# Cache loads of a decoder step's sample attention issued by ScalarE's queue instead of SyncE's

## What is computed

```python
n   = rms_norm(x) @ w_in                      # 320 x 2048 @ 2048 x 4608, nine blocks of 512 columns
ya  = u * (tril(w_s) @ rms_norm(v))           # gMLP gate
yb  = window_attention(q, [cache_k, k], [cache_v, v], rel_bias)   # 16 heads x 64, three dilations mixed
ym  = memory_attention(qm, mk, mv)            # 4 heads x 128, 256 memory tokens
h   = x + concat(ya, yb, ym) @ w_out
y   = h + moe(rms_norm(h))                    # top-1 of 4 groups, top-2 of 8 SwiGLU experts in it
```

## Time and profile before

| | us |
|---|---|
| median of 3 runs | 1200.65 |
| the runs | 1200.0, 1200.65, 1203.96 |
| the profiled execution, its own time | 1201.35 |
| its span, first to last instruction | 1199.5 |
| mean granted TensorE clock | 0.963 |

### The profile page before, as it was taken

One profiled execution on the slowest core, in us unless ns is written; L12 is line 12 of the kernel. 1 busy time (PEld: TensorE's weight loads), 2 busy tenths in 40 slices (PEclk: granted clock), 3 DMA queues, 4 the chain that ended last, 5 costly groups with the idle time before them and its releaser, 6 DMA issues.

```text
span 1199.5 us, 17462 instructions
## 1 busy us (share of the span) xinstructions
PE 1076.0 (90%) x7153; PEld 593.7 (49%) x7153; DVE 534.4 (45%) x1046; ACT 212.0 (18%) x465; POOL 41.4 (3%) x38
## 2 busy tenths in 40 slices
PE   7996889998999999989999998898888878888876
PEld 3674667665676665767777542333222222222322
DVE  3573553556455455475354215334242433333323
ACT  1111011231122221231011023111211210101010
POOL 0030110001010000010000000000000000000000
PEclk9897899999999999999999999999999998999997
DMA  9987234898999998753773436999999999999994
GB/s 334 337 243 295 97 128 146 357 369 316 370 351 392 403 371 316 312 220 105 271 284 132 176 134 267 428 425 427 427 428 427 428 428 428 427 427 427 426 426 149
DMA packets 38751, 385.48 MB, mean 321 GB/s; under 512 B 4879, under 2 KB 7567, under 8 KB 10223
## 3 DMA queue, kind: packets, MB, share of 16 engines
q1 hardware_dynamic: 36112, 376.87, 78.6%
q0 software_dynamic: 1568, 5.62, 1.7%
q10 hardware_dynamic: 1008, 2.10, 0.5%
HBM read 376.67 MB, written 7.90 MB: 321 GB/s over the span
## 4 chain that ended last, share of the span: by engine, by line
PE 65%; DMA 20%; DVE 7%; issue 3%; ACT 3%; POOL 1%; DVEq 0%; SPq 0%; ACTq 0%; POOLq 0%
PE ps L594 22%; DMA arena<-w_gu 16%; PE ps L586 6%; PE ps L1007 5%; PE ps L1037 5%; DMA arena<-w_proj 4%; PE ps L990 4%; PE ps L1021 3%; PE ps L788 3%; PE ps L755 3%; PE ps L576 3%; PE ps L1014 2%; PE ps L1042 1%; POOL stat L1798 1%; PE ps L771 1%
## 5 line engine op out<-in xcount | busy, mean ns | idle before, releaser
L594 PE MATMUL ps<-arena 128*128 128x256 f32 x1456 | 343.0, 391 | 22.4 <-DMA arena<-w_proj 12.3
L594 PEld LDWEIGHTS ps<-arena 128*128 128x128 f32 x1456 | 276.5, 194 | 76.6 <-issue 28.3
L1007 PE MATMUL ps<-arena,cst 128*32 128x512 f32 x1024 | 130.4, 643 | 40.3 <-DMA arena<-w_gu 39.4
L1749 DVE STREAM_TRANSPOSE cst<-ps 128x512 f32<-128x512 f32 x31 | 22.2, 717 | 192.8 <-PE ps L990 192.8
L586 PE MATMUL ps<-arena 128*64 128x256 f32 x832 | 101.3, 385 | 0.0
L990 PE MATMUL ps<-arena 128*32 128x512 f32 (+1 forms) x768 | 95.7, 612 | 1.2 <-DVE arena L1698 1.2
L1007 PEld LDWEIGHTS ps<-arena,cst 128*32 128x32 f32 x1024 | 32.7, 114 | 128.5 <-issue 84.1
L1021 PE MATMUL ps<-arena,cst 128*32 128x512 f32 x512 | 68.1, 653 | 20.7 <-DVE cst L1751 20.7
L586 PEld LDWEIGHTS ps<-arena 128*64 128x64 f32 x832 | 55.1, 136 | 38.4 <-issue 14.8
L1767 DVE COPY arena<-ps 32x512 f32<-32x512 f32 x64 | 44.2, 691 | 51.9 <-PE ps L1021 51.0
L1292 DVE TENSOR_TENSOR arena<-arena 128x512 f32<-128x512 f32 x52 | 35.7, 687 | 67.7 <-PE ps L594 45.8
(11 more groups left out here) (262 smaller groups left out, 974.5 us busy)
## 6 DMA issues: line engine op xcount, KB each, us to landing
arena<-w_gu SPq DMA_DIRECT2D x64, 2048.0 KB, 32.6
arena<-w_dn SPq DMA_DIRECT2D x32, 2048.0 KB, 31.2
arena<-w_proj SPq DMA_DIRECT2D x43, 1024.0 KB, 7.8
arena<-kc SPq DMA_DIRECT2D x16, 2048.0 KB, 9.9
arena<-vc SPq DMA_DIRECT2D x16, 2048.0 KB, 9.7
arena<-w_o SPq DMA_DIRECT2D x16, 1024.0 KB, 4.9
arena<-kc SPq DMA_DIRECT2D x8, 1024.0 KB, 8.1
arena<-vc SPq DMA_DIRECT2D x8, 1024.0 KB, 9.6
```

The costliest lines, as they stand in the source:

```text
L594: last = mm(psum[:, regions(v)[j - 1]], left[a], right[:, a], start=first and opens and a == 0, stop=final and a == 1, skip_group_check=True)
L1007: last = mm(ps[g:g + 32, 0, :], xgT[:, s % 2, kt, :], gate_up[(3 * s + h) % RING][:, k, :], start=kt < 4, stop=kt >= KT - 4)
```

## The change

The functions keys and values move from SyncE's program into ScalarE's, with the same semaphores, sources, sizes and destinations; the 48 loads are issued by ScalarE's queue. In ScalarE's tile loop the calls stand behind sample_exp and sample_turned and ahead of the memory attention, head_turned and turned. Unit 0's three key loads are written at s = 5, behind a wait for the 16 pieces of the memory projection. SyncE keeps weights, biases, rows and expert weights, and loses the two waits (sumsq, unit_done) that stood ahead of unit 0's keys.

```diff
@@ SyncE's program
-            def keys(n, j):
-                if n:
-                    sp.wait_ge(spv_mm, 3 * n - 2 + j)
-                a = HP * sum(KEYS_P[:j])
-                sp.dma_start(kp[j], kc[n, :, a:a + HP * KEYS_P[j]]).then_inc(kv_loaded[j], 16)
-
-            def values(n, j):
-                sp.wait_ge(s_mm, 3 * n + j + 1)
-                a = HP * sum(KEYS_P[:j])
-                sp.dma_start(vp[j], vc[n, :, a:a + HP * KEYS_P[j]]).then_inc(kv_loaded[j], 16)
-
             sp.wait_ge(tab_out, 16)
             window_bias(0)
             window_bias(1)
             sp.wait_ge(rows_out, 16 * NQ)
             sp.wait_ge(dset, 2)
             sample_bias(0)
-            sp.wait_ge(sumsq, 5)
-            sp.wait_ge(unit_done, UNITS_M)
-            for j in range(3):
-                keys(0, j)

             for s in range(UNITS_X):
                 if s % 3 == 2:
                     sp.wait_ge(unit_done, UNITS_M + s + 1)
                     weights(11 + s // 3)
-                n, i = sample_step(s)
-                if n is not None and i <= 2:
-                    values(n, i)
-                if n is not None and i >= 4 and n + 1 < NUNIT:
-                    keys(n + 1, i - 4)
@@ ScalarE's program
+            def keys(n, j):
+                if n:
+                    act.wait_ge(spv_mm, 3 * n - 2 + j)
+                a = HP * sum(KEYS_P[:j])
+                act.dma_start(kp[j], kc[n, :, a:a + HP * KEYS_P[j]]).then_inc(kv_loaded[j], 16)
+
+            def values(n, j):
+                act.wait_ge(s_mm, 3 * n + j + 1)
+                a = HP * sum(KEYS_P[:j])
+                act.dma_start(vp[j], vc[n, :, a:a + HP * KEYS_P[j]]).then_inc(kv_loaded[j], 16)
+
             for s in range(UNITS_X):
+                if s == 5:
+                    act.wait_ge(unit_done, UNITS_M)
+                    for j in range(3):
+                        keys(0, j)
                 if s % 12 == 10:
                     evict_first(s // 12)
                 if s % 12 == 11:
@@
                 if n is not None and 3 <= i <= 5:
                     sample_turned(n, i - 3)
+                if n is not None and i <= 2:
+                    values(n, i)
+                if n is not None and i >= 4 and n + 1 < NUNIT:
+                    keys(n + 1, i - 4)
                 if s in (MEM_AT, MEM_AT + 2):
                     memory_exp((s - MEM_AT) // 2)
```

## The result

The changed kernel takes 1203.94 us in the median of 12 runs (1197.89 to 1205.36), the kernel before 1200.22 us in 12 runs beside them (1198.6 to 1203.96). The ratio is 1.0025, with a 95% interval of 1.0014 to 1.0036: slower by about 3 us, when 1198.65 was forecast and 1203.0 was the end of the range. The profiled execution has a span of 1203.0 us, 3.5 us over the one before.

The account below looks back on a forecast made before the run. PE bounds the kernel until the expert stage, where DMA does. A 2.7 us gain at chunk 11 less 0.7 us of issues gave -2.0 us: 1199.35 for the profiled execution, 1198.65 us as median; range 1187.5 to 1203.

Parts of the forecast that it names:

- What bounds the kernel, and the stop at 95.5 us: PE's work sets the pace before the expert stage; in tile 9 PE waits 11.5 us for chunk 11, behind the keys.
- rival (a): Full relief before tile 9: stores and SyncE's queue hardly slowed, chunk 11 in time, 13.6 us gained, 1187.75 us; chance 0.20.
- The keys go out at 74 to 75 us, not at tile 5: ScalarE stands idle from 73.94 us until tile 9, so unit 0's key loads go out 11 us earlier than before.
- The gain of 2.7 us from the 76 to 84.3 us stretch: Keys use spare DMA room there; chunk 11 lands near 104.2 us, PE waits 8.8 us; gain 2.7 us, bounds 0.7 to 4.2.
- since everything else ahead of chunk 11 stays: In SyncE's queue, the keys gain only what they move from 76 to 84.3 us without pushing the rest back.
- The bias rows' stores: SyncE waits for them before the samples' bias and chunk 11; their end was expected after 82.76 but before 90 us.
- The issues cost ScalarE 1.0 us: Unit 0's three key issues before tile 9 take 3 x 0.334 us of ScalarE's idle time, costing nothing.
- The 45 loads of the loop: Moving these to ScalarE gains 0; their issues take 15 us, mostly covered, and their later landing is priced at 0.
- the 0.7 us charged for these two waits: In the tile loop, two waits of PE for ScalarE each lengthen by one 0.33 us key issue.
- rival (c): Slower: in tiles 43 to 90 keys reach qk late once loads exceed about 12 us; 1207.3 us, half of it 1203; chance 0.18.
- (b), no relief: Before tile 9 the keys hold back the bias rows, chunk 11 stays where it was; 1201.4 us, bounds 1200.5 to 1202; chance 0.17.
- 0.65 on relief: Chances that early keys bring chunk 11 sooner: partial relief, the forecast, 0.45, and full relief 0.20.

Follow-up runs that it names:

- three: The changed kernel, with unit 0's three key loads issued by ScalarE in tile 13 behind a wait for tile 11: 1187.14 us, ratio 0.9886.
- four: The kernel before, all loads on SyncE's queue, with unit 0's keys issued behind chunk 15 in tile 14: 1187.15 us, ratio 0.9890.
- nine: The changed kernel, keys still early, with only the samples' bias loads moved to tile 14: 1195.3 us, ratio 0.9946.
- ten: The kernel before, all loads on SyncE's queue, with only the samples' bias loads moved to tile 14: 1196.05 us, ratio 0.9957.
- sixth kernel: The changed kernel, with unit 0's keys on ScalarE's queue also waiting for the bias rows' stores (rows_out): 1202.44 us, ratio 1.0011.
- eleventh kernel: The changed kernel, with unit 0's keys behind rows_out on ScalarE's queue and the samples' bias behind chunk 11 (tile 2): 1193.69 us, ratio 0.9934.
- kernel two: The changed kernel, with unit 0's three key loads back on SyncE behind the samples' bias, the other 45 on ScalarE: 1201.68 us, ratio 1.0014.
- first kernel: The kernel before, with only unit 0's three key loads moved to ScalarE's queue, the other 45 staying on SyncE: 1203.59 us, ratio 1.0024.

## Why the prediction was wrong

**What bounds the kernel, and the stop at 95.5 us: right.** With the keys away from chunk 11 the stop and the slow matmuls are gone and 13.5 us with them (three, four); 13.6 us was the price that rival (a) gave to that.

**The keys go out at 74 to 75 us, not at tile 5: right, to within 2 us** (from 72.4 us), and it is why the change doesn't help. Where it was worded as tile 5, it acts before tile 0 is done. Had the issue really been tied to PE's progress past tile 11, it would have been the third kernel.

**The gain of 2.7 us from the 76 to 84.3 us stretch: right in size, wrong as a gain.** 1.2 MB more moved in it, 2.9 us of work, net of the 0.7 MB of stores and loads that the keys put off. The step that failed is the clause it rested on, "since everything else ahead of chunk 11 stays". The sum took what lay behind 84.3 us as work that goes at its old rate in any mixture. It doesn't: next to the samples' bias, loads that fill only 64 of 128 partitions each, the keys were slowed with it, 272 GB/s from 88 to 98 us where the kernel before had 380, and 1.0 MB less was moved from 84.3 to 107 us. Chunk 11 landed at 108.2 us, not at 104.2. The nine and ten pair shows that the bias has this part: 9.5 us beside the keys, 5.2 ahead of them. Without it the forecast gain is there in PE's wait, 5.0 us for 8.0; in the medians it is 1.3 us and not clear of noise. Why the bias slows its neighbour is open. The half-filled partitions are one possible reason; the bias loads' pieces of 32 bytes (L448), or their reading rows that had only just been stored, are others, and none was tried.

**The bias rows' stores.** The prediction saw that SyncE waits for them, and its cases ran from no delay to an end beyond 93 us. They ended 2.6 us later. The sixth kernel says that this isn't what decides: with rows_out back at 82.5 us, and the keys issued only then, chunk 11 is as late.

**The issues cost ScalarE 1.0 us: wrong** (7.26 us for two of the three), harmless there, as nothing stands behind them until tile 9.

**The 45 loads of the loop.** No wait of PE for caches, as forecast. PE's waits from 205 to 575 us, with the old L755 as L735, L788 as L768, L710 as L690:

```profile
PE ps L735 <- issue: 3.6, 1, 3.6
PE ps L709 <- DVE arena L1427: 3.1, 3, 1.4
PE ps L768 <- ACT arena L1132: 2.0, 1, 2.0
PE ps L751 <- ACT arena L1124: 1.5, 2, 0.9
PE ps L690 <- ACT arena L1119: 1.1, 1, 1.1
```

L768 and L690 still wait 2.0 and 1.1 us, so the 0.7 us charged for these two waits was too much: in this execution they aren't longer. The key loads' own rows have one weight load of PE waiting 0.3 us, which is all there is of rival (c), and its 12 us limit wasn't reached in the median (median landing 10.1 us for the 2 MB loads, 9.9 before):

```profile
L1141 ACTq DMA_DIRECT2D arena<-kc x24: 334/334/3702, 72.4 to 471.0; - x24
...
  PEld ps L735: 0.3, 1
```

**The rivals.** What happened is (b), no relief, and a little worse: 1201.4 was its price and 1202 its upper bound, which left out that mixing can cost. The gap to 1203.94 is the term missing from both. The Trainium skill, page "DMA: Bandwidth & Descriptors", section "Issuing engines are not separate DMA queues", says that loads interleave on the same 16 engines whichever engine issues them. That gave the better forecast, and the trace agrees with it: in the eleventh kernel the two queues' shares are 67.7% and 36.2%, together all of the 16 engines. That (b) had only 0.17, with 0.65 on relief, was the misjudgement of the chances.

What stays open: what it is in the samples' bias that slows the keys, how the lower granted clock near 180 and 285 us comes about, whether the loop's moves cost the 0.2 to 3 us that kernel two shows (three against four can't tell), and whether one megabyte fits for nothing.

## What to carry to other kernels

A load that isn't due should be issued behind those that are, by a wait that ties it to the consumer's progress; moving it to another queue doesn't take it out of their way, since both queues share the 16 engines (67.7% and 36.2% in the eleventh kernel). A line in a tile loop of an engine that has nothing else to do there runs long before that tile: put the wait in. And before counting idle room in a stretch as gain, look at what the moved bytes will share the engines with: here 1.2 MB were won in eight microseconds and nearly all lost again in the next 23.

## What the runs showed of the hardware

- A busy share of 1.0 says nothing of the rate. Mixtures ran at 241 to 305 GB/s from 88 to 98 us (the first kernel, the changed one, the sixth), a mixture of keys and chunks at 418 (the ninth), each with the engines at 1.01 to 1.03.
- A load can slow another queue's load that shares the engines with it. The same keys took 2.4 us of the 16 engines per MB beside stores or weights (changed kernel, 76 to 84.3 us; ninth, 88 to 98) and 3.6 us per MB beside the samples' bias (changed kernel, 88 to 98 us; 80.3% of 10 us for 2.47 MB in the sixth is 3.3, 58.5% for 1.41 MB in the first is 4.1).
- With two queues at work, a 1 MB load took 13.5 us beside 5.24 MB of the other, for 4.7 us alone, and the other queue had two thirds of the engines (eleventh kernel, where more loads followed in the first queue).
- Issuing a load can take long: up to 3.7 us for one issue on ScalarE while the DMA engines were backed up (changed kernel), for 0.33 us in the median.
